# Reading the moving operand of every projection in runs of eight tokens from two halves of its row

## The reference

```python
for l in range(DEPTH):                                # DEPTH = 2
    h = rms_norm(x, g_mix[l])
    z = h @ w_in[l]                                   # 1024 -> 10752
    ya = retention(rotary(qa), rotary(ka), va)        # 4 heads, then head norm and swish gate
    yb = spatial_gating(gelu(ub), gelu(vb), ...)      # 4 channel groups
    yc = three dilated window attentions, combined    # 12 heads
    merged = sum over 3 branches of sigmoid(gate_b) * (y_b @ w_branch[l, b])
    x = x + merged @ w_o[l]
    h = rms_norm(x, g_ffn[l])
    gate, up = split(h @ w_gate_up[l])                # 1024 -> 2 x 2816
    x = x + (silu(gate) * up) @ w_down[l]
```

## Time and profile before

| | |
|---|---|
| median of two runs | 2071.1 us |
| span of the profiled execution | 2066.1 us |
| TensorE matmuls busy | 2032.9 us |
| VectorE busy | 1125.0 us |
| ScalarE busy | 752.1 us |
| GpSimd busy | 10.5 us |
| moved by DMA | 192 MB, 93 GB/s on average |

### The profile page before, as it was taken

How to read it: one execution, slowest core, us unless ns; L and a number is a source line. 1 busy time by engine, 2 the same in 40 slices (tenths; PEclk the granted TensorE clock), 3 DMA queues, 4 the chain that set the end, 5 groups by cost and what they waited for, 6 DMA issues and landing times. The chain is left out here.

```text
span 2066.1 us, 27744 instructions
## 1 busy us (share of the span) xinstructions
PE 2032.9 (98%) x9368; PEld 1682.6 (81%) x9368; DVE 1125.0 (54%) x1516; ACT 752.1 (36%) x1090; POOL 10.5 (1%) x11
## 2 busy tenths in 40 slices
PE   7999999999999999999999999999999999999999
PEld 6888887788888888888878788877888888888887
DVE  6656657645555443344465666576365554433444
ACT  4444444433234322232334443344332343222333
POOL 2000000000000000000000000000000000000000
PEclk9999999999999999999999999999999999999999
DMA  5222222222232232323222222222222322323233
GB/s 181 84 73 72 72 72 92 87 92 92 92 117 98 92 102 92 102 92 99 86 94 77 62 82 72 78 92 82 92 94 90 123 92 92 102 92 100 94 96 119
DMA packets 65474, 192.02 MB, mean 93 GB/s; under 512 B 17200, under 2 KB 17456, under 8 KB 65328
## 3 DMA queue, kind: packets, MB, share of 16 engines
q1 hardware_dynamic: 65328, 190.17, 28.8%
HBM read 187.98 MB, written 2.16 MB: 92 GB/s over the span
## 5 line engine op out<-in xcount | busy, mean ns | idle before, releaser
L661 PE MATMUL bank<-h_high,w_high 128*128 128x512 f32 x2048 | 811.4, 396 | 15.0 <-DVE w_low L993 10.0
L661 PE MATMUL bank<-h_high,w_low 128*128 128x512 f32 x2048 | 800.4, 391 | 0.0
L661 PE MATMUL bank<-h_low,w_high 128*128 128x512 f32 x2048 | 799.4, 390 | 0.0
L827 ACT ACTIVATE w_high<-raw 128x1024 fp32r<-128x1024 f32 x342 | 362.4, 1060 | 1039.0 <-PE bank L661 1035.5
L661 PEld LDWEIGHTS bank<-h_high,w_high 128*128 128x128 f32 x2048 | 386.3, 189 | 95.9 <-issue 15.9
L993 DVE TENSOR_TENSOR w_low<-raw,w_high 128x1024 fp32r<-128x1024 f32 x342 | 416.7, 1221 | 66.9 <-ACT w_high L827 49.7
L661 PEld LDWEIGHTS bank<-h_high,w_low 128*128 128x128 f32 x2048 | 385.7, 188 | 81.8
L661 PEld LDWEIGHTS bank<-h_low,w_high 128*128 128x128 f32 x2048 | 386.3, 189 | 78.7
L661 PE MATMUL bank<-in_high,w_high 128*128 128x512 f32 x672 | 261.8, 390 | 0.0
L661 PE MATMUL bank<-in_low,w_high 128*128 128x512 f32 x672 | 261.5, 389 | 0.0
L661 PE MATMUL bank<-in_high,w_low 128*128 128x512 f32 x672 | 261.5, 389 | 0.0
(11 more groups left out here) (108 smaller groups left out, 1070.7 us busy)
## 6 DMA issues: line engine op xcount, KB each, us to landing
raw<-weights SPq DMA_DIRECT2D x343, 512.0 KB, 3.4
row<-rows SPq DMA_DIRECT2D x3, 768.0 KB, 4.7
xT<-x_t SPq DMA_DIRECT2D x8, 256.0 KB, 5.8
decay_sb<-decay SPq DMA_DIRECT2D x8, 256.0 KB, 3.9
out_t<-xT SPq DMA_DIRECT2D x8, 256.0 KB, 5.7
sgw<-spatial SPq DMA_DIRECT2D x3, 256.0 KB, 2.6
rot<-rotation SPq DMA_DIRECT2D x1, 512.0 KB, 7.9
pairs_by_token<-pairs SPq DMA_DIRECT2D x16, 4.0 KB, 5.1
```

The costliest lines, as they stand in the source:

```text
L661: return pe.matmul(o, w, m, start=start, stop=stop)
L827: act.activation(w_high[:, PART_SLOT[s], :, :], raw[:, s % RAW_SLOTS, :, :], ACT.Copy).then_inc(part_high_w.sem, 1)
```

## The change

Each row of 512 tokens of `h_high`, `h_low`, `in_high` and `in_low` is stored in another order. The tokens are taken as 64 runs of eight. The even runs go to the first 256 places of the row, the odd runs to the last 256. The matmul's moving operand reads the row back in the order of tokens: eight from the first half, eight from the second, and so on (`in_turn`). A run is 32 bytes, the halves are 1024 bytes apart. The outputs, the weights and everything behind the matmul are as before. `row_sq` (rows of `in_high` and `in_low` that hold squares) is written and read as before.

The writers change with it. ScalarE's copy reads its source as runs (`parted`) and writes the two halves (`halves`), in one instruction as before. VectorE's subtraction for in does the same. Its low part for h becomes two instructions, one for each half, and the second one raises `low_ready`.

```diff
+        def in_turn(stored):
+            return stored.rearrange("p (a c t) -> p c a t", a=2, t=8)
+        def parted(tokens):
+            return tokens.rearrange("p (c a t) -> p a c t", a=2, t=8)
+        def halves(stored):
+            return stored.rearrange("p (a c t) -> p a c t", a=2, t=8)
...
-                    matmul(o[:, :], wh, hi, n == 0, False)
-                    matmul(o[:, :], wh, lo, False, False)
-                    last = matmul(o[:, :], wl, hi, False, n == len(blocks) - 1)
+                    matmul(o[:, :], wh, in_turn(hi), n == 0, False)
+                    matmul(o[:, :], wh, in_turn(lo), False, False)
+                    last = matmul(o[:, :], wl, in_turn(hi), False, n == len(blocks) - 1)
...
-                act.activation(dst, xT[:, n, :], ACT.Copy, scale=gain[:, n:n + 1]).then_inc(high_ready.sem, 1)
+                act.activation(halves(dst), parted(xT[:, n, :]), ACT.Copy, scale=gain[:, n:n + 1]).then_inc(
+                    high_ready.sem, 1)
...
-                        act.activation(parts(key)[0], src, ACT.Copy).then_inc(high_ready.sem, 1)
+                        act.activation(halves(parts(key)[0]), parted(src), ACT.Copy).then_inc(high_ready.sem, 1)
...
-                dve.scalar_tensor_tensor(dst, xT[:, n, :], gain[:, n:n + 1], high, ALU.mult, ALU.subtract).then_inc(
-                    low_ready.sem, 1)
+                for a in range(2):
+                    last = dve.scalar_tensor_tensor(halves(dst)[:, a, :, :], parted(xT[:, n, :])[:, a, :, :],
+                                                    gain[:, n:n + 1], halves(high)[:, a, :, :], ALU.mult, ALU.subtract)
+                last.then_inc(low_ready.sem, 1)
...
-                        dve.tensor_tensor(lo, src, hi, ALU.subtract).then_inc(low_ready.sem, 1)
+                        dve.tensor_tensor(halves(lo), parted(src), halves(hi), ALU.subtract).then_inc(low_ready.sem, 1)
```

## The result

The changed kernel takes 2192.1 us (median of two runs, 2191.7 and 2192.6) against 2071.1 before. The ratio is 1.0585, with a 95% interval of 1.0555 to 1.0614. The forecast was 1987, and its range ended at 2105.

The account below looks back on a forecast made before the run. The prediction took the step of TensorE's projection matmuls to bound the kernel. Terms of -91 + 0.2 + 1.5 + 5 = -84 us gave a span of 1982 and a time of 1987 us; the range went from 1965 to 2105.

Parts of the forecast that it names:

- the step of a projection matmul is the kernel's time: TensorE: 8160 projection matmuls, 226.7 ns from start to start, make 1850 us, 90% of the span.
- the 13.3 ns: Projection matmul step: the part of 226.7 ns above 213.3 ns of streaming, read as moving operand and weight load meeting in SBUF.
- The no-change rival: Projection matmuls: the order of reading does not matter, the step stays 226.7 ns; 2073 us, chance 0.26.
- readers at one speed meet once and then stay apart: SBUF reads of TensorE: reading from two halves brings moving operand and weight load to about the same speed, ending their meetings.
- If the meeting goes, the step falls to what the same streaming time costs in the f32 form: Projection matmuls: the step falls from 226.7 to 215.5 ns, saving 91 us over 8160 matmuls.
- Steps behind transposes that are even from the second on: TensorE's timeline after transposes: a sign of being right, where steps before were uneven with a mean of 231 ns.
- A step above 226.7 with even values: Projection matmuls in TensorE's timeline: a sign of being wrong, meaning a price per run.
- I take nothing for a break, because here a run is eight elements long: Moving operand's reading: breaks between runs cost 0; at 0.76 ns each, 64 breaks would be 49 ns a matmul, +398 us.
- The slower rival: Projection matmuls: a weight load that meets the moving operand keeps meeting it; step 240 ns, 2182 us, chance 0.22.
- All three cases: Projection matmul step: full gain or most of it (0.45), no change (0.26), slower (0.22).
- The small terms: Side costs: +0.2 us at the program's end, +1.5 us in the prologue, 0 for ScalarE's copies; half a low part 477 ns.
- Given back: TensorE's waits on other engines: a 5% faster TensorE reaches them earlier, +5 us, between 0 and 15.

Follow-up runs that it names:

- e7: Kernel before, plain rows, with the weights read in steps of 8 bytes, so products are of mixed weights: 2114.6 us.
- e12: Kernel before, plain rows; the matmul reads runs of eight in steps of 128 bytes, so output tokens stand in another order: 2032.2 and 2050.8 us.
- e14: Kernel before, plain rows, with weight blocks 544 instead of 512 bytes apart, same values and result: 2103.6 us.
- e6: Kernel before, 64 instead of 128 weight columns for the second and third matmul in all blocks but a tile's last: 2086.0 us, ratio 1.0081.
- e8: Changed kernel with the weights read in steps of 8 bytes, so products are of mixed weights: 2190.0 us.
- e17: Changed kernel with weight blocks 544 instead of 512 bytes apart, same values and result: 2184.7 us.
- e2: Changed kernel with runs of 16 tokens instead of eight, in storage and in the matmul: 2166.3 us.
- e3: Changed kernel with runs of 4 tokens instead of eight, in storage and in the matmul: 2242.1 us.
- e5: Changed kernel with runs of 64 tokens instead of eight, in storage and in the matmul: 2070.4 us.
- e11: Kernel before, plain rows; the matmul reads runs of eight in steps of 256 bytes, so output tokens stand in another order: 2275.8 us.
- e13: Kernel before, plain rows; the matmul reads runs of eight in steps of 128 bytes and writes PSUM in the same order: 2049.0 us, median of four.
- e16: Kernel before, with the second matmul of each block taking 384 of the 512 tokens: 1969.8 us, one run.

## Why the prediction was wrong

**That the step of a projection matmul is the kernel's time** held. Of the 124 us that the span grew, the step is 128; later starts and shorter waits make up the difference.

**That the 13.3 ns are a matter of the order of addresses** held as far as it went. The earlier trace rows had suggested it, and e7, e12 and e14 show it: each changes only addresses, on one side or the other, and the step moves to 233.3, 220.0 and some 231 ns. That the 13.3 ns are meetings of two readers is not shown: e6 gave two of three loads half the columns (134 instead of 188 ns as recorded), and the step grew by 2.7 ns. The no-change rival rested on a rule of the Trainium skill ("SBUF — State Buffer", section "Who interferes with whom"), that TensorE's two reads are independent. e14 does not fit it: the loads were recorded as long as before, and moving them still moved the step. And the rule is silent on what the order of one read costs by itself, which is where the loss came from.

**The step that failed** is the next one: "readers at one speed meet once and then stay apart", and with it the term "If the meeting goes, the step falls to what the same streaming time costs in the f32 form". Reading from two halves was to halve the pace over low address positions and free the moving operand from the weight load. Instead the new order costs the moving operand time by itself: 30.0 ns over the 213.3 of streaming instead of 13.3, from the first step after an interruption on, and untouched by the weights' order (e8) or place (e17). I had built a picture of one conflict, between two readers, and asked only what the change does to that one. The order of the moving operand alone can be bad, and nothing in my picture priced that. Two of the prediction's signs also misled. Steps behind transposes that are even from the second on were to be a sign of being right; they came (241 to 246 ns), with the loss. A step above 226.7 with even values was to mean a price per run, which e2, e3 and e5 refute.

**"I take nothing for a break, because here a run is eight elements long"** is the term in which this hides. Its far end, 0.76 ns a break from VectorE's by-phase write, was worth 49 ns; the value measured is 16.7 ns for 63 changes in this order. But a price per break is the wrong form: 63 changes cost +6.7, -6.7, +32, +4.4 or +16.7 ns, depending on the distance, and 7 changes to the far half cost nothing (e5). Neither does a rule on short pieces help. The Trainium skill's "SBUF — State Buffer", section "Door 1: The DMA port swizzle", says that lines of 16 bytes want at least two hits each; every order here takes all four values of a line, even e3's, and the steps still go from 220 to 259 ns.

**The slower rival** named 2182 us and 240 ns; 2192.1 and 243.3 were measured. Its number was good and its mechanism was not: two readers that stay together should have parted in e8 or e17, which change the weights' pace and place. Its 240 ns came near by luck. It had a chance of 0.22, and the range stopped at 2105, short of it. All three cases turned on an unseen property of one instruction, and a range that leaves out one whole side of them was too narrow.

**The small terms** were near. A half of a low part takes 480 ns (477 worked out). ScalarE's copies and VectorE's subtractions in runs of eight keep their time. The prologue's low parts take 863 ns a half, 1726 a pair instead of 1523, and TensorE's wait for low parts of h grew from 0.7 to 2.4 us. The first sum-of-squares matmuls start at 22.21 us instead of 19.55, 1.0 us of which the first matmul was late already; 1.5 was taken and at most 2 named as a sign. "Given back" had the right sign for the opposite case: a slower TensorE got 9 us of waits back.

**What stays open** is what the moving operand meets when it is slowed by its own order. The runs exclude one price per change of run, a cost of pieces under 64 bytes alone, one threshold in distance, and that the weights' order or place sets the step with halves. They don't show the mechanism. The same holds for the plain order's 13.3 ns, and for what makes a stretch of e11 or e13 enter one rhythm or another.

## What to carry to other kernels

When a settled matmul step is some per cent above columns over clock, try the order of reading and measure it; don't reason it out. Permuting the moving operand and the PSUM output in the same way left every token in place, and in e13 cost nothing else that showed. Judge each order by the distance between starts in several long stretches, since one kernel can hold two rhythms and keep the worse one for 1559 matmuls. And a change whose whole effect is one unmeasured property of one instruction, times 8160, deserves a small run of that instruction before it is built.

## What the runs showed of the hardware

The step of an fp32r matmul of 512 columns at the upper clock level is not fixed. With the same columns, weights and clock it was 220.0, 226.7, 231.1, 233.3, 236.7, 240.0, 243.3, 246.7, 250.0 or 258.9 ns, by the order in which the moving operand's runs are read. Except for 231.1 and 258.9, all of these are whole multiples of 3.33 ns (66, 68, 70, 71, 72, 73, 74 and 75), four ticks of 1.2 GHz. One order can settle at more than one value: runs of eight in steps of 256 bytes at 233.3, 258.9 or 263.3 ns, in steps of 128 bytes at 220.0 or 230.7. Loads or matmuls of unequal size in the sequence (e6, e16) break the even pattern and lengthen the steps of the others.

At the lower clock level none of this shows. The earlier trace rows has 426.7 ns for plain rows, which is 512 columns at 1.2 GHz (the trace has no record of the clock that early). The changed kernel, in a stretch in which the trace does record half the clock (0.50 granted from 1106.3 to 1108.8), reads:

```profile
1106.32 0.63 PE L672 MATMUL bank<-h_high,w_high 128*128 128x512 f32 x1
...
1108.88 0.52 PE L672 MATMUL bank<-h_high,w_high 128*128 128x512 f32 x1
```

Six steps in 2.56 us are 426.7 ns again. In such stretches of all twenty kernels the settled steps of 512 columns are 426 to 428 ns, e3's and e11's too.

Plain row order is not the best order. Runs of eight in steps of 128 bytes run at 220.0 ns where they catch the right rhythm, 3% below the plain 226.7.
